# Feed-forward input of a hybrid layer: tokens as the stationary operand, 512 outputs a job, on one core

## The reference

```python
def conv_ffn(u, w_ffn_in, ffn_conv_w, ffn_conv_b, w_ffn_out):     # D_FF = 5632
    gate, val = jnp.split(u @ w_ffn_in, 2, axis=-1)               # w_ffn_in: 2048 x 11264
    h = jax.nn.gelu(causal_dwconv(gate, ffn_conv_w, ffn_conv_b), approximate=False) * val
    return h @ w_ffn_out                                          # three taps; w_ffn_out: 5632 x 2048
...
u = rms_norm(h, ffn_norm_w[i])
h = h + conv_ffn(u, ...)
return rms_norm(h, final_norm_w)
```

## Time and profile before

| | us |
|---|---|
| median of 3 runs | 1923.75 (1923.60 to 1923.87) |
| the profiled execution | 1923.14 |
| its span | 1921.4 |
| TensorE busy | 1910.4 (99%) |
| VectorE busy | 1308.0 (68%) |
| ScalarE busy | 1083.7 (56%) |
| GpSimd busy | 38.0 (2%) |
| mean granted TensorE clock | 0.999 of full speed |

### The profile page before, as it was taken

The page is one execution under the profiler, slowest core; times in us unless marked ns, Lnnn a source line. Parts: engine busy times, 40 slices in busy tenths (PEclk is TensorE's granted clock), DMA queues, the critical chain, the costliest instruction groups (busy, mean ns, idle before and its releaser), DMA issues.

```text
span 1921.4 us, 28874 instructions
## 1 busy us (share of the span) xinstructions
PE 1910.4 (99%) x10205; PEld 1624.1 (85%) x10205; DVE 1308.0 (68%) x1634; ACT 1083.7 (56%) x1478; POOL 38.0 (2%) x79
## 2 busy tenths in 40 slices
PE   9999999999999999999999999999999999999998
PEld 7888888888888878888888888888888888888886
DVE  6787788777878874645544778666666766645444
ACT  6566765677657764444344445666666666534443
POOL 1000000000010100000000000000000000000000
PEclk9999999999999999999999999999999999999999
DMA  7666666656654446666666576666666666566564
GB/s 248 198 187 186 187 195 190 190 170 196 206 160 137 131 127 213 196 189 195 196 190 194 186 240 207 188 186 195 188 192 190 186 186 193 188 198 195 192 194 143
DMA packets 294902, 361.52 MB, mean 188 GB/s; under 512 B 13168, under 2 KB 218032, under 8 KB 293424
## 3 DMA queue, kind: packets, MB, share of 16 engines
q1 hardware_dynamic: 294832, 360.59, 61.2%
HBM read 358.38 MB, written 2.16 MB: 188 GB/s over the span
## 4 chain that ended last, share of the span: by engine, by line
PE 99%; issue 0%; DMA 0%; DVE 0%; ACT 0%; SPq 0%; POOLq 0%; POOL 0%; DVEq 0%; ACTq 0%
PE ps L1485 36%; PE ps L1487 18%; PE ps L1470 14%; PE ps L1471 14%; PE ps L1472 14%; PE ps L1683 1%; PE ps L1611 1%; PE ps L1624 1%; PE ps L1635 0%; PE ps L1684 0%; PE ps L1672 0%; PE ps L1527 0%; PE ps L1562 0%; PE ps L1636 0%; PE ps L1668 0%
## 5 line engine op out<-in xcount | busy, mean ns | idle before, releaser
L901 DVE TENSOR_TENSOR lo<-raw,hi 128x1024 fp32r<-128x1024 f32 x652 | 796.2, 1227 | 467.6 <-ACT hi L466 461.6
L1485 PE MATMUL ps<-uHL,hi 128*128 128x512 f32 x2944 | 1035.3, 396 | 0.0
L466 ACT ACTIVATE hi<-raw 128x1024 fp32r<-128x1024 f32 x652 | 682.8, 1055 | 511.3 <-PE ps L1472 379.7
L1487 PE MATMUL ps<-uHL,lo 128*128 128x256 f32 x2944 | 823.9, 280 | 0.0
L1485 PEld LDWEIGHTS ps<-uHL,hi 128*128 128x128 f32 x2944 | 551.7, 187 | 130.5 <-issue 5.4
L1487 PEld LDWEIGHTS ps<-uHL,lo 128*128 128x128 f32 x2944 | 555.9, 189 | 0.0
L1472 PE MATMUL ps<-hi,aL 128*128 128x512 f32 x384 | 149.5, 389 | 0.0
L1472 PE MATMUL ps<-hi,hL 128*128 128x512 f32 x352 | 136.9, 389 | 0.0
L1471 PE MATMUL ps<-lo,hH 128*128 128x512 f32 x352 | 136.9, 389 | 0.0
L1470 PE MATMUL ps<-hi,hH 128*128 128x512 f32 x352 | 136.9, 389 | 0.0
L476 ACT ACTIVATE hb<-ps 128x512 f32<-128x512 f32 x92 | 54.8, 595 | 121.5 <-PE ps L1487 121.5
(11 more groups left out here) (204 smaller groups left out, 1695.3 us busy)
## 6 DMA issues: line engine op xcount, KB each, us to landing
raw<-w_in SPq DMA_DIRECT2D x261, 512.0 KB, 4.2
raw<-w_ffn_in SPq DMA_DIRECT2D x176, 512.0 KB, 3.8
raw<-w_ffn_out SPq DMA_DIRECT2D x88, 512.0 KB, 4.4
raw<-w_ssm_out SPq DMA_DIRECT2D x64, 512.0 KB, 4.2
raw<-w_attn_out SPq DMA_DIRECT2D x32, 512.0 KB, 4.4
raw<-w_o SPq DMA_DIRECT2D x32, 512.0 KB, 4.5
rows_b<-cum_rows SPq DMA_DIRECT2D x8, 1024.0 KB, 6.7
x_tok<-x SPq DMA_DIRECT2D x8, 256.0 KB, 5.4
```

Source lines behind the costliest of these rows:

```text
L466: act.activation(hi[:, s % SLOTS, :], raw[:, s % SLOTS, :], ACT.Copy).then_inc(hi_ready, 1)
L901: ve.tensor_tensor(lo[:, s % SLOTS, :], raw[:, s % SLOTS, :], hi[:, s % SLOTS, :].bitcast(F32), ALU.subtract).then_inc(lo_ready, 1)
L1485: pe.matmul(ps[:, pair + c, :], w_hi, uHL[:, kk].rearrange("p a n -> p (a n)"), start=kk == 0, stop=False)
L1487: last = pe.matmul(ps[:, pair + c, 0:SEQ], w_lo, uHL[:, kk, 0, :], start=False, stop=kk == k - 1)
```

## The change

Gate and value are now computed with `rows` units: 11 iterations `f` of 16 units, 8 for 512 gates (pair A) and 8 for 512 values (pair B). ScalarE takes each result from PSUM with the token's reciprocal root as the scale (`gate_tok`, `value_tok`; `rstd` has tokens on partitions, so it isn't turned any more). VectorE turns them to channels with 16 transposes of 32-row blocks each, two at a unit: gates after units 11 to 15 and 0 to 2 of the next iteration, values after units 3 to 10. The taps run on four channel tiles. GpSimd multiplies the gelu by the value. The output stage wants the last `hL` at unit 20. `fw` is loaded in the output stage, where `yw` lay, and its wait stands before its first use.

```diff
 U_O = U_M + M_UN * M_IT - 8
-U_F, F_UN, F_IT = U_O + 32, 8, FF // W2
+U_F, F_UN, F_IT = U_O + 32, 16, FF // W5
...
         h1, a = place("h1", [P, TT, D], a)
-        fw, a = place("fw", [P, D], a)
-        gv, a = place("gv", [P, 2, SEQ], a)
-        ht, a = place("ht", [P, 2, SEQ], a)
-        sqo, a = place("sqo", [P, W5], a)
-        gs, a = place("gs", [P, 2, SEQ], a)
+        gate_tok, a = place("gate_tok", [P, TT, W5], a)
+        gv, a = place("gv", [P, 4, SEQ], a)
+        ht, a = place("ht", [P, 4, SEQ], a)
+        gs, a = place("gs", [P, 4, SEQ], a)
         assert a <= region + 120 * KB
-        yw, _ = place("yw", [P, TT, D], u_at)
+        value_tok, _ = place("value_tok", [P, TT, W5], region + (2 * KF - 4) * KB)
+        sqo, _ = place("sqo", [P, W5], region + 120 * KB)
+        yw, a = place("yw", [P, TT, D], u_at)
+        fw, _ = place("fw", [P, D], a)
...
-            sp.dma_start(fw[:], fnorm.to_broadcast([P, D])).then_inc(fw_landed, 16)
             with sp.Fori(0, F_IT) as f:
                 d = f * F_UN
-                columns(U_F, d, "fi", f * W2, KD)
-                columns(U_F + 4, d, "fi", f * W2 + FF, KD)
-            with sp.Fori(0, E_IT) as e:
-                for j in range(2):
-                    rows(U_E + (KF // 2) * j, e * E_UN, "fo", e * (2 * W5) + j * W5, KF)
+                rows(U_F, d, "fi", f * W5, KD)
+                rows(U_F + 8, d, "fi", f * W5 + FF, KD)
+            for j in range(4):
+                for i in range(KF // 2):
+                    if j == 0 and i == 8:
+                        sp.wait_ge(unit_used, U_E)
+                        sp.dma_start(fw[:], fnorm.to_broadcast([P, D])).then_inc(fw_landed, 16)
+                    stream(U_E + (KF // 2) * j + i, 0, "fo", 2 * i, 2, j * W5, W5)
...
             root(2)
+            with po.Fori(0, F_IT) as f:
+                po.wait_ge(values_turned, f + 1)
+                po.wait_ge(gelu_ready, f + 1)
...
+            def gate_tokens(f):
+                act.wait_ge(unit_used, f * F_UN + (U_F + 8))
+                for t in range(TT):
+                    last = act.activation(gate_tok[:, t, :], ps[:, A + t, :], ACT.Copy, scale=rstd[:, t:t + 1])
+                last.then_inc(pair_free[A], 1)
+
+            def value_tokens(f):
+                act.wait_ge(unit_used, f * F_UN + (U_F + F_UN))
+                for t in range(TT):
+                    last = act.activation(value_tok[:, t, :], ps[:, B + t, :], ACT.Copy, scale=rstd[:, t:t + 1])
+                last.then_inc(pair_free[B], 1)
+
             def gate_start(f):
-                act.wait_ge(gs_ready, f + 1)
-                for i in range(2):
+                act.wait_ge(gates_turned, f + 1)
+                for i in range(4):
                     act.activation(gv[:, i, :], gs[:, i, :], ACT.Identity,
-                                   scale=pcol("ffn_conv_w", f * (2 * FTAPS) + (i * FTAPS + FTAPS - 1)),
-                                   bias=pcol("ffn_conv_b", f * 2 + i)).then_inc(fconv_first, 1)
+                                   scale=pcol("ffn_conv_w", f * (4 * FTAPS) + (i * FTAPS + FTAPS - 1)),
+                                   bias=pcol("ffn_conv_b", f * 4 + i)).then_inc(fconv_first, 1)
...
 
             def h_hi(f):
                 act.wait_ge(ht_ready, f + 1)
+                act.activation(hH[:, ds(f * 4, 4), :], ht[:], ACT.Copy).then_inc(hh_ready, 1)
+
+            def h_before(f, u):
+
+                if u == 2:
+                    value_tokens(f)
+                if u == 4:
+                    gate_start(f)
+                if u == 9:
+                    gelu(f)
+                if u == 13:
+                    h_hi(f)
+
+            act.wait_ge(rstd_ready, 2)
+            for u in range(SLOTS, F_UN):
+                hi_of(U_F + u, 0)
+                if u == 10:
+                    gate_tokens(0)
...
-                    if u == 0:
-                        gelu(f - 1)
-                    if u == 2:
+                    h_before(f - 1, u)
+                    if u == 10:
+                        gate_tokens(f)
...
             mean(4)
-            spread(2)
             norm_lo("ffn_norm", KD, 3)
-            def h_of(f):
-                scaled(ht[:], B, f * 2 + (H_F + 2))
-                ve.drain()
-                ve.wait_ge(gelu_ready, f + 1)
-                ve.tensor_tensor(ht[:], ht[:], gv[:], ALU.mult).then_inc(ht_ready, 1)
+            def tokens_turned(dst, src, n):
+
+                q, r = n // (P // B32), n % (P // B32)
+                to = dst.rearrange("p i (t n) -> p i t n", t=TT)
+                of = src.rearrange("p t (i n) -> p i t n", i=4)
+                return ve.transpose(to[r * B32:(r + 1) * B32, :, :, q * B32:(q + 1) * B32],
+                                    of[q * B32:(q + 1) * B32, :, :, r * B32:(r + 1) * B32])
+
+            def gate_turn(f, n):
+                if n == 0:
+                    ve.drain()
+                    ve.wait_ge(pair_free[A], f + (J_OA + 1))
+                for i in range(2):
+                    last = tokens_turned(gs[:], gate_tok[:], n + i)
+                if n == 14:
+                    last.then_inc(gates_turned, 1)
+
+            def value_turn(f, n):
+                if n == 0:
+                    ve.drain()
+                    ve.wait_ge(pair_free[B], f + (J_OB + 1))
+                for i in range(2):
+                    last = tokens_turned(ht[:], value_tok[:], n + i)
+                if n == 14:
+                    last.then_inc(values_turned, 1)
+
+            def conv(f, tap, i0):
+                if tap:
+                    ve.drain()
+                else:
+                    ve.wait_ge(fconv_first, f * 4 + 4)
+                sh = FTAPS - 1 - tap
+                for i in range(i0, i0 + 2):
+                    last = ve.scalar_tensor_tensor(out=gv[:, i, sh:SEQ], in0=gs[:, i, 0:SEQ - sh],
+                                                   scalar=pcol("ffn_conv_w", f * (4 * FTAPS) + (i * FTAPS + tap)),
+                                                   in1=gv[:, i, sh:SEQ], op0=ALU.mult, op1=ALU.add)
+                if tap == FTAPS - 2 and i0:
+                    last.then_inc(fconv_done, 1)
...
-                ve.tensor_tensor(hL[:, ds(f * 2, 2), :], ht[:], hH[:, ds(f * 2, 2), :].bitcast(F32),
+                ve.tensor_tensor(hL[:, ds(f * 4, 4), :], ht[:], hH[:, ds(f * 4, 4), :].bitcast(F32),
+            def h_before(f, u):
+
+                if u < 3:
+                    gate_turn(f, 10 + 2 * u)
+                elif u < 11:
+                    value_turn(f, 2 * (u - 3))
+                if 5 <= u < 9:
+                    conv(f, (u - 5) // 2, 2 * ((u - 5) % 2))
+                if u == 15:
+                    h_lo(f)
+
+            for u in range(SLOTS, F_UN):
+                lo_of(U_F + u, 0)
+                if u >= 11:
+                    gate_turn(0, 2 * (u - 11))
+                    h_before(f - 1, u)
+                    if u >= 11:
+                        gate_turn(f, 2 * (u - 11))
...
                     if u % half == 5 and n:
+                        if n == 1:
+                            ve.wait_ge(fw_landed, 16)
...
-                if u == 4:
+                if u == 8:
                     pe.wait_ge(panel_added, 4)
-                    turn_rstd(2)
-                columns(U_F + u, 0, (A, B)[u // 4], KD, 4 * (u % 4), 4,
-                        before=(lambda kk: pe.wait_ge(u_ready, KD + kk + 1)) if u == 3 else None)
+                rows(U_F + u, 0, (A, B)[u // 8], U, KD, 2 * (u % 8),
+                     before=(lambda kk: pe.wait_ge(u_ready, KD + kk + 1)) if u in (6, 7) else None)
                 for u in range(F_UN):
                     if u == 0:
                         job(A, f + J_OA)
-                    if u == 4:
+                    if u == 8:
                         job(B, f + J_OB)
-                    columns(U_F + u, f * F_UN, (A, B)[u // 4], KD, 4 * (u % 4), 4)
...
-                    if n == 0 and u >= half - 1:
+                    if n == 0 and u >= half - 2:
```

More of the change, by code:

```diff
@@ L92 @@
 H_Q = H_X + 2
-H_F = H_Q + 2 * (KVH - 1)
 PC = {}
@@ L260, in build @@
         merged, m_turned, mh_ready, ml_ready = sem("merged"), sem("m_turned"), sem("mh_ready"), sem("ml_ready")
-        gs_ready, fconv_first, fconv_done, gelu_ready = (
-            sem("gs_ready"), sem("fconv_first"), sem("fconv_done"), sem("gelu_ready"))
+        gates_turned, values_turned = sem("gates_turned"), sem("values_turned")
+        fconv_first, fconv_done, gelu_ready = sem("fconv_first"), sem("fconv_done"), sem("gelu_ready")
         ht_ready, hh_ready, hl_ready = sem("ht_ready"), sem("hh_ready"), sem("hl_ready")
@@ L454, in _ @@
             root(2)
+            with po.Fori(0, F_IT) as f:
+                po.wait_ge(values_turned, f + 1)
+                po.wait_ge(gelu_ready, f + 1)
+                po.tensor_tensor(ht[:], ht[:], gv[:], ALU.mult).then_inc(ht_ready, 1)
             root(3, 0, 1)
@@ L880, in _ @@
```

(46 more changed lines are left out.)

## The result

| us | before | after |
|---|---|---|
| median of 6 runs each | 1923.61 | 1913.93 |
| span of the profiled execution | 1921.4 | 1911.6 |
| TensorE busy | 1910.4 | 1900.9 |
| VectorE busy | 1308.0 | 1401.7 |
| ScalarE busy | 1083.7 | 1056.1 |

The ratio of the medians is 0.9949, with a 95% interval of 0.9939 to 0.9959: 9.7 us faster. The forecast was 1914.1.

The account below looks back on a forecast made before the run. TensorE, almost never waiting, bounds the kernel through its matmuls' number and distance. The stage falls from 489.3 to 479.7 us, other work hidden: 1923.14 - 9.6 = 1913.5 profiled, 1914.1 us on the runs' scale; range 1912.5 to 1920.0.

Parts of the forecast that it names:

- TensorE, 9.6 us: Feed-forward input: 12 matmuls a unit instead of 16, 13 ns fixed part each; stage 489.3 to 479.7 us.
- rival C: Feed-forward input: matmuls come no closer, a unit keeps 2.77 us; 1923.5 us, or 1922.0 with 2.5 ns fixed; chance 0.03.
- Hidden work: Feed-forward input: the other engines' work stays behind TensorE, with no wait or a few tenths an iteration; chance 0.84.
- VectorE's sum: VectorE's work per 16 units: 39.6 of 43.5 us, with 2.3 us more lost to the collision with GpSimd.
- its busy share: VectorE's busy share in the feed-forward input stage, near 90 to 96%.
- A pair of taps: Two taps on VectorE in units 5 to 8, priced at 0.96 us.
- the multiply: GpSimd's 128x1024 multiply of gelu and value: 2.6 us alone, costing VectorE 2.3 us in collision.
- Unit 11's reserve: Unit 11 of each iteration: its `lo` split ends 2.0 us before TensorE wants it.
- the two signs of the collision: One `lo` split in sixteen of about 3.5 us, or GpSimd's multiply over 3 us.
- What a rival would need: VectorE late at unit 11: beyond 2.0 us delay each us costs 11; 1930.6 (chance 0.08), in small 1920.7 (0.05).
- The last edits: Wider input-weight packets landing in 4.4 us instead of 3.8, and the final norm's moved load: both hidden.
- the lower end: Fastest time of the forecast range, 1912.5 us, if matmuls come 1 ns closer still.

Follow-up runs that it names:

- the form alone: Kernel before, with only TensorE's feed-forward input run as token-stationary units of 12 matmuls of 512 columns: 1914.14 us.
- the halves: Changed kernel, with the matmuls of 84 of the output stage's 88 units split into two of 256 columns, except the first of each sum: 1927.34 us.
- the old form put back: Changed kernel, with only TensorE's feed-forward input returned to weight-stationary units of 8 pairs of 512 and 256 columns: 1923.22 us.
- The third transposes: Changed kernel, with VectorE repeating one value transpose after each pair at units 3 to 10: 1921.90 us; with gate transposes repeated too: 1958.32 us.
- Half of the repeats: Changed kernel, with VectorE repeating one value transpose only at units 3 to 6: 1913.54 us.
- four multiplies: Changed kernel, with GpSimd multiplying the value by the gelu four times in place instead of once: 1958.91 us.
- the groups with the new form: Changed kernel, with TensorE's x and z columns of the 8 Mamba groups (128 units) also as token-stationary units: 1904.38 us.

## Why the prediction was right

- **TensorE, 9.6 us.** Forecast 479.7 us for the stage, measured 479.6. The term is shown from both sides: the form alone gives the gain in the kernel before (479.9 us), and its removal takes it away (489.1). That it is a fixed part for each matmul, and not the form, is shown by the halves. The two distances of the old form lie outside this account: it fits since the pairs of the feed-forward input all stood at the shorter one, which the prediction had measured in that very stage.
- **The Trainium skill's 2.5 ns** ("TensorE: Matmul & The Clock Gate", section "Wait — 56ns, not 53.3ns?"; rival C's figure) does not hold for these float32r matmuls. The form alone, the old form put back and the halves all give 13 ns.
- **Hidden work.** Right in the result, with prices that were too high, so on the safe side. VectorE's sum was forecast as 39.6 + 2.3 = 41.9 us and is 40.9; its busy share is 89%, just under the 90 to 96 that the prediction named. A pair of taps takes 0.88 plus at times 0.17, not 0.96 each time; the multiply takes 2.41 instead of 2.6, and costs VectorE 1.47 instead of 2.3, since it starts 0.8 us before the split it meets. Unit 11's reserve was forecast as 2.0 and is 3.0. Neither of the two signs of the collision came as named: the split took 2.70 us instead of about 3.5, and ten of eleven multiplies took 2.41, not over 3.
- **What a rival would need.** Here a step of the prediction failed. I took the reserve at unit 11 (2.0, later 3.0 us) as what decides, with 11 us for each us beyond. The third transposes showed another limit: VectorE's sum against the 43.5 us of an iteration, with 2.6 us to spare. With eight repeats 0.89 us was lost in an iteration (44.41 - 43.52). With a repeat at its measured 0.51 us the chain up to unit 11 gives 7 x 0.51 - 3.0 = 0.6, the sum 0.9; VectorE had no wait for `hi` left, which it would have kept if the chain alone had set the pace; and TensorE stopped at units 9 and 12, not at 11. Half of the repeats cost nothing. In these runs the order within an iteration decided only where an engine stood at a wait with needed work behind it, as with four multiplies.
- **The last edits.** The loads of the input weight with wider packets land in 4.1 us (before 3.8) and nobody waits for them; the load of the final norm's weight neither.

- **Slips in the working.** (489.31 - 0.87 - 0.22) / 1408 is 0.3467 and not 0.3466, and matmuls 1 ns closer would have given 1912.0 as the lower end, not 1912.5. Neither moves the forecast.

Not settled: why the fixed part is 13 ns, and what sets the two distances of the old form.

## What to carry to other kernels

Where TensorE is the bound and never waits, count its matmuls. Here the same columns in fewer instructions gained 13 ns for each one saved, and this could be read off two stages with different forms before anything was built. Measure the distance in the stage that you change: a unit of the groups gave back 1.21 / 16 = 0.076 us, one of the feed-forward input 0.055. The work that moved to other engines was free until VectorE's sum reached the time of an iteration, so add up the fullest list first, collisions between VectorE and GpSimd included. Then look for waits in a list with needed work queued behind them: such waits can cost before the sum does, and TensorE's stop of 2.85 us here cost its clock as well.

## What the runs showed of the hardware

- At the full clock a matmul of 256 columns takes 0.120 us and one of 512 takes 0.2267, both with a weight load of their own of some 0.19 us, which stays hidden.
- The pair of 512 and 256 columns lasts 0.3467 in some stretches and 0.3533 in others, in the same program with the same operands' shapes; it changes only where other matmuls come between. In the kernel before, a group's pairs go from 0.3533 to 0.3467 at 209.6 us, where the means are taken, and stay at 0.3533 at the same place of the next group, at 270.7. Stretches of 512-column matmuls alone show no such thing: 0.2267 in the feed-forward stages, 0.2267 to 0.2271 in the groups with the new form.
- With four multiplies TensorE began no matmul for 2.85 us, and its granted clock fell to the 1.2 GHz level: the next eight matmuls took 3.42 instead of 1.81 us.
- GpSimd's multiply of 128x1024 float32 took 2.41 us, and 3.43 where it met a running split and had to wait for it. The split behind it waits in its turn, but VectorE's transposes don't: beside the multiply from 1389.74 to 1393.17, in the run with a third value transpose, two of them took 0.88 us, as they do alone.
